# One core, two transformer stacks: attention's banks, order and row sums, and how the norms sum over tokens

## What is computed

```python
def softmax_attend(q, k, v, scale):
    s = jnp.einsum('bhqd,bhkd->bhqk', q, k, preferred_element_type=jnp.float32) * scale
    p = jax.nn.softmax(s, axis=-1)
    return jnp.einsum('bhqk,bhkd->bhqd', p.astype(v.dtype), v)
...
# 8 heads, 128 + 64 (rotary) wide; the 256 latent queries see 512 keys, the 256 context queries see 256
o_l = sweep_query_blocks(lambda qb: softmax_attend(qb, k_all, v_all, scale), q_l)
q_c = jnp.concatenate([qn_c, qr_c], axis=-1)
out_c = merge_heads(softmax_attend(q_c, k_c, v_c, scale)) @ w_o
...
def layer_norm(x, g, b):
    mu = jnp.mean(xf, -1, keepdims=True)
    var = jnp.mean(jnp.square(xf - mu), -1, keepdims=True)
    return ((xf - mu) * lax.rsqrt(var + LN_EPS) * g + b)
# and rms_norm(x, w), the same without the mean
```

## Time and profile before

| | us |
|---|---|
| median of 3 runs | 3162.78 (3161.76 to 3164.16) |
| profiled execution, its own time | 3161.56 |
| its span | 3159.8 |
| attention, first score to the start of `mla_o` | 1928.48 to 2048.14, 119.66 |
| PE busy in it | 105.28 |
| mean granted clock in it | 0.83 of full |

### The profile page before, as it was taken

How to read it: one execution, slowest core, us unless ns; L and a number is a source line. 1 busy time by engine, 2 the same in 40 slices (tenths; PEclk the granted TensorE clock), 3 DMA queues, 4 the chain that set the end, 5 groups by cost and what they waited for, 6 DMA issues and landing times.

```text
span 3159.8 us, 49212 instructions
## 1 busy us (share of the span) xinstructions
PE 2994.7 (95%) x21883; PEld 1920.0 (61%) x21883; DVE 713.7 (23%) x1261; ACT 405.0 (13%) x768; POOL 448.1 (14%) x320
## 2 busy tenths in 40 slices
PE   5999999978989999999998898889999999999999
PEld 3866878843475555556555433444444454798888
DVE  2304210077530000000001285410000012351100
ACT  0032010010111000000001242310000011121000
POOL 0013019347500000000000171000000000250000
PEclk7999999977789999999999896989999999999999
DMA  8576454437727999999997110012222222212442
GB/s 277 148 267 238 133 154 147 161 117 273 270 86 266 362 379 380 383 374 383 382 380 282 36 61 5 14 54 69 78 80 73 73 67 80 94 54 80 147 147 91
DMA packets 363785, 564.41 MB, mean 179 GB/s; under 512 B 43684, under 2 KB 196300, under 8 KB 363468
## 3 DMA queue, kind: packets, MB, share of 16 engines
q1 hardware_dynamic: 341436, 556.79, 50.6%
q10 hardware_dynamic: 22160, 4.77, 0.8%
HBM read 557.31 MB, written 1.05 MB: 177 GB/s over the span
## 4 chain that ended last, share of the span: by engine, by line
PE 50%; issue 35%; POOLq 5%; POOL 2%; DVE 2%; DMA 2%; DVEq 1%; ACT 1%; SPq 1%; ACTq 1%
PE psum L744 11%; PE psum L1383 10%; PE psum L1262 5%; PE psum L1399 5%; POOLq L2650 3%; PE psum L791 3%; PE psum L855 2%; PE psum L1425 2%; PE psum L1010 2%; DMA prow<-in_s_log_dt 1%; PE psum L773 1%; POOLq L2740 1%; PE psum L1452 1%; PE psum L805 1%; PE psum L1059 1%
## 5 line engine op out<-in xcount | busy, mean ns | idle before, releaser
L1131 PE MATMUL psum<-ring,xe 128*32 128x256 f32 x8448 | 465.7, 380 | 0.0
L744 PE MATMUL psum<-act_in,ring 128*128 128x256 f32 x1920 | 423.8, 382 | 14.7 <-DMA ring<-in_ffn_w 7.1
L744 PEld LDWEIGHTS psum<-act_in,ring 128*128 128x128 f32 x1920 | 366.8, 192 | 68.1 <-issue 10.5
L1131 PEld LDWEIGHTS psum<-ring,xe 128*32 128x32 f32 x8448 | 269.8, 110 | 182.4 <-issue 8.4
L1383 PE MATMUL psum<-a,ring 128*128 128x512 f32 x704 | 305.3, 597 | 8.7 <-DVE a L2457 8.7
L1383 PEld LDWEIGHTS psum<-a,ring 128*128 128x128 f32 x704 | 134.8, 192 | 178.7 <-issue 178.7
L1155 PE MATMUL psum<-ring,zs 128*32 128x256 f32 x4224 | 238.2, 381 | 4.9 <-ACT zs L1739 4.9
L1262 PE MATMUL psum<-a,ring 128*128 128x512 f32 (+1 forms) x480 | 212.0, 604 | 4.8 <-ACT a L1776 4.1
L1155 PEld LDWEIGHTS psum<-ring,zs 128*32 128x32 f32 x4224 | 138.3, 110 | 96.1 <-issue 6.9
L2395 DVE TENSOR_TENSOR zs<-zs,psum 128x128 f32<-128x128 f32 x132 | 37.8, 288 | 644.1 <-ACT zs L1735 644.1
L1262 PEld LDWEIGHTS psum<-a,ring 128*128 128x128 f32 (+1 forms) x480 | 91.9, 192 | 123.3 <-issue 120.6
(11 more groups left out here) (390 smaller groups left out, 3179.3 us busy)
## 6 DMA issues: line engine op xcount, KB each, us to landing
ring<-in_moe_w SPq DMA_DIRECT2D x320, 512.0 KB, 7.1
ring<-in_ffn_w SPq DMA_DIRECT2D x98, 1024.0 KB, 5.2
ring<-in_ada_w SPq DMA_DIRECT2D x96, 1024.0 KB, 7.2
ring<-in_moe_w SPq DMA_DIRECT2D x88, 1024.0 KB, 8.6
ring<-in_hg_w_in SPq DMA_DIRECT2D x20, 1024.0 KB, 5.0
ring<-in_mlstm_w_in SPq DMA_DIRECT2D x16, 1024.0 KB, 5.8
ring<-in_moe_w SPq DMA_DIRECT2D x64, 256.0 KB, 5.8
ring<-in_mlstm_w_out SPq DMA_DIRECT2D x8, 1024.0 KB, 6.3
```

What stands on the lines that cost most here:

```text
L744: last = pe.matmul(bank(j)[:, n * T:(n + 1) * T], tile[:, k * width + n * P:k * width + (n + 1) * P], src(k), start=start and k == 0, stop ...
L1131: last = pe.matmul(psum[32 * g:32 * g + 32, r, 0:2 * P].rearrange("p (u n) -> p u n", u=2), xe[:, 2 * i + k, at:at + 32], tile[:, k, :, g ...
```

## The change

It has four parts.

1. The scores leave the rotating banks. S(h, k) writes bank 3 (h mod 2) + k, six banks in all; T always uses bank 6 and O bank 7. A score tile of head h waits for the exponential of head h-2 in its bank; a turning waits until the turning before it has been copied out.
2. PE's order becomes S(h+1, k), T(h, k) for k = 0, 1, 2, with O(h-1) behind T(h, 0). ACT follows the same sequence. DVE takes the maximum of tile n and then scales tile n-1.
3. The row sums of the probabilities come from ACT's exponential (`accum_out`), and DVE's sum over `prob` (2495) goes.
4. `token_sums` takes ones (128x32) as the stationary operand and a chunk's squares as the moving one, 256 or 512 columns wide. Chunk c goes to the 32 array columns (c mod 4), so four partial sums stand on partitions 0, 32, 64 and 96 (each repeated 32 times). ACT copies them to `part_sums`, and PE adds the four by a product of each block of 128 tokens with a column that is one at those four partitions. That takes one more job and one more bank, so ln has 4 jobs and rms 3.

```diff
-    for h in range(AH + 1):
-        if h + 1 < AH:
-            seq += [("S", h + 1, k) for k in range(3)]
-        if h < AH:
-            seq += [("T", h, k) for k in range(3)]
-        if h >= 1:
-            seq.append(("O", h - 1, 0))
-    return seq
+    for h in range(AH):
+        for k in range(3):
+            if h + 1 < AH:
+                seq.append(("S", h + 1, k))
+            seq.append(("T", h, k))
+            if k == 0 and h:
+                seq.append(("O", h - 1, 0))
+    return seq + [("O", AH - 1, 0)]
...
-            def token_sums(j, src, blocks, ready, first=True):
-
+            def token_sums(j, src, n, ready):
+
+                wait_free(pe, j)
                 for c in range(DC):
                     ready(c)
-                    for a in blocks:
-                        last = pe.matmul(bank(j)[:, a:a + 1], src(c, a), ones[:, 0:1], start=first and c == 0 and a == blocks[0],
-                                         stop=c == DC - 1, skip_group_check=True)
-                return last
+                    g = 32 * (c % 4)
+                    last = pe.matmul(bank(j)[g:g + 32, 0:n * P], ones[:, 0:32], src(c), start=c < 4, stop=c >= 4)
+                full(last, j)
+                wait_free(pe, j + 1)
+                wait_out(pe, j)
+                for a in range(n):
+                    last = pe.matmul(bank(j + 1)[:, a:a + 1], part_sums[:, a * P:(a + 1) * P], c_("partial")[:, 0:1],
+                                     start=True, stop=True)
+                full(last, j + 1)
...
                     if kind == "S":
-                        wait_free(pe, j)
-
+                        if h >= 2:
+                            pe.wait_ge(S("prob_exp"), 3 * (h - 2) + k + 1)
+                        scores = score_bank(h, k)
...
                         pe.wait_ge(S("prob_ready"), 3 * h + k + 1)
-                        turn(j, [prob[:, h % 2, k, s * P:(s + 1) * P] for s in range(4)])
+                        if 3 * h + k:
+                            pe.wait_ge(S("probT_out"), 3 * h + k)
+                        for s in range(4):
+                            last = pe.transpose(psum[:, P_TURNED, s * P:(s + 1) * P], prob[:, h % 2, k, s * P:(s + 1) * P], ident)
+                        last.then_inc(S("probT_full"), 1)
...
+            def sums_out(j, n):
+                wait_full(act, j)
+                out_of(act.activation(part_sums[:, 0:n * P], bank(j)[:, 0:n * P], ACT.Copy), j)
...
-                                                  ACT.Exp, bias=smax[:, h % 2, 2 * k + a:2 * k + a + 1], scale=ATT_SCALE)
-                        out_of(last, j)
+                                                  ACT.Exp, bias=smax[:, h % 2, at:at + 1], scale=ATT_SCALE,
+                                                  accum_out=smax[:, h % 2, 8 + at:9 + at])
+                        last.then_inc(S("prob_exp"), 1)
...
+                for n in range(3 * AH):
+                    row_max(n)
+                    if n:
+                        scale_rows(n - 1)
+                scale_rows(3 * AH - 1)
```

100 lines of the change are left out of this document (52 added, 48 removed).

## The result

The changed kernel takes **3115.22 us** (median of 4 runs, 3114.8 to 3118.55), the kernel before 3162.59 in the same comparison (3161.76 to 3164.16): ratio 0.986, 95% interval 0.9847 to 0.9872. The direction was as forecast. The gain, 47 us, was far above the 28 forecast and outside the range.

What follows compares the result with a forecast made beforehand. PE, busy 95% of the span, was taken as the bound. Gains of 9.8 us in the attention and 17.4 in the norms, 27.2 off the profiled 3161.56, gave 3134.4, left at 3134.5; range 3121 to 3145.

Steps and rivals of the forecast that it cites:

- Stalls and the last copy: Attention: PE's remaining waits for copies and the last exponential, 5.4 us, plus 0.7 for the last copy.
- What is late next: Attention: T(h, 0) waits for ACT's copy of the turning before, behind the exponential, 0.1 to 0.3 us a head.
- the low clock at the start: Attention's start: time lost at half speed before PE's clock rises, 18.4 us in place of 15.0.
- the 4.7 and the 6.1: Attention's start: us to the clock's rise, after turnings began (4.7) and in an unbroken run of wide 128-row products (6.1).
- the first long run: Attention: T(1, 0) with O(0), beginning 31.8 us after the first score, with the clock's rise put 5 us later.
- Rival (a): Attention: four turnings and the score behind them raise the clock at 21.3 us; kernel 3127, chance 0.18.
- run half their time on 64 rows with gaps: Attention's start: remark on scores at the low clock, beside 25.2 us of scores not raising it.
- The norms: Token sums in the norms: shorter path behind the last square to the root or clearing, 17.4 us gained in all.
- the range's low end: Whole kernel: 3121, from rival (a) with free row sums, ln0's clearing at full clock earlier, and 1 for error.
- The sums on ACT: Attention: the exponential also writing its row sum costs ACT 0.1 us, counted within the stall of 0.2 a head.

Runs made afterwards that it cites:

- full_rows: Changed kernel with head 0's second score product reading the 128-row content queries and keys instead of the 64-row rotated ones; 3106.09 us, ratio 0.9828.
- wide_runs: Changed kernel with the two products of every second score tile in the other order, so 128-row products stand in pairs; 3111.20 us, ratio 0.9848.
- norms_only: Kernel before with the norms' part of the change alone; 3134.86 us, ratio 0.9927.

## Why the prediction was wrong

**The order and the waits held.** Stalls and the last copy were put at 5.4 + 0.7; they are 3.9 + 0.7 + 0.7 = 5.3. T(h, 0) waits 0.16 a head, inside the 0.1 to 0.3 of the working, and the period is PE's work. What is late next was rightly named.

**The term that failed is "the low clock at the start", 18.4.** It came out at 9.5 (half of 19.0), plus 1.7 in the output at the end, which I had not foreseen: 7.2 less. Of the attention's gain of 18.6 I had put 8.3 on waits, which gave 9.1, and 1.5 on the clock, which gave 8.7. The step was "I put the rise 5 us later, between the 4.7 and the 6.1, at 36.8", built on the first long run behind which the rise would come. In the changed kernel the rise came at 19.0 without such a run, behind four turnings and one 128-row product. Rival (a) had the size nearly right, 21.3. Its mechanism is half borne out: the rise does come right behind the first turnings of probabilities, but twelve turnings added earlier didn't bring it forward, so turnings alone don't raise it. Why these are enough stays open. The pointer that I had and didn't use was in my own sentence that scores "run half their time on 64 rows with gaps": full_rows and wide_runs show that the alternation is what keeps the scores at the low clock, and that the rise comes at 5.4 and 8.8 us where it is broken.

**The norms: path right, clock left out.** Where the sums run at the full clock, the working holds to a few tenths: ln1 to ln3 3.3 for 3.2, rms1 3.9 for 3.9. Three places are larger. ln0 gave 3.6 for 0.9: I took only the earlier start of the clearing, while it also ran at the full clock (3.68 for 6.50); I had kept that for the range's low end. rms0 gave 6.5 for 4.7: its eight one-column products took 1.02, at the full clock, where I had reckoned 8 x 0.215 at the low one. The trace has the rest: 0.5 ahead of the squares, where the spreading of ln3 takes 0.71 for 1.22, and 0.5 between the last square and the copy (1.64 for 2.1). And 2.2 behind rms0 and 1.4 on the way to rms2 came in work that I had taken as only shifted: it shifted, but its clock rose sooner. By the medians of norms_only it is 24.8 for 17.4. So the clock was the miss in the norms too: most of the 8 us over the forecast, in the account's rows, is time at the full clock that I had counted at the low one.

**The sums on ACT** were put at 0.1 a tile; a read takes 0.19, and the four of a head cost 0.16 on the path. The size was small either way, but the sign of this part was never asked: it costs.

**Chance**, some 8 us either way in a feed-forward and in the S5 stage, was not in the forecast. In the two profiled runs it nearly cancels.

## What to carry to other kernels

A low-clock stretch is a term of its own, here 11.2 us against 5.3 of waits: ask what PE runs there, not only how long. Here 13.8 us of one-column products and 7.0 us of 64x64 ones ran at the low level throughout, twelve added transposes brought no rise, and 128-row products alternating with 64-row ones stayed low for 25 us. Pairing the full ones gave 6.6 us of attention without added work, and throw-away products in an idle gap ahead gave 10.8 for 0.7.

When several readers share one engine's queue, interleave the producer's work finely before adding buffers: six banks with the old order made the attention 19.5 us longer.

Before moving work off a path because an engine "has room", look at what stands behind it in that engine's queue; and of an exposed table load, ask what runs beside it.

## What the hardware showed

- Products on 128 and on 64 rows in alternation, without a wait, stayed at the 1.2 GHz level for 25.2 us; the same products in pairs reached 2.4 GHz after 8.8 us, 128-row ones alone after 5.4.
- From start to start a 256-column product took 0.63 us at the full clock where the rows alternate, 0.43 behind one of the same rows; 2.00 and 1.71 with 512 columns at the low clock.
- With sixteen products of zeros ahead of the attention its scores, which alternate as before, began and stayed at 2.4 GHz.
- Twelve added turnings, of the identity or of data, moved the rise from 19.0 to 22.4 us; products of the same number and shape moved it to 8.7.
- An exponential that also gives its row sum is followed by a read of 0.19 to 0.20 us on ACT.
- While two loads of 8 KB in single values were under way (ACT waited 34 us for them), the 1 MB weight loads of another queue moved 0 GB/s in one run and 113 in another; with them at the start of the program PE waited 42 us for its first weights, and the kernel took 32 us more.
